# GpSimd's low part of a weight slot: one subtraction of 2048 columns, or four of 512

## The reference, cut to what matters

```
h = rmsnorm(x);  proj = h @ w_in
y_a = rwkv7_time_mix(proj...);  y_b = short_conv(proj...);  y_c = dilated_attention(proj...)
merged = sum_i sigmoid(gate_i) * (y_i @ w_branch[rows_i]);  x += rmsnorm(merged @ w_out)
x += rmsnorm((silu(h @ w_gate) * (h @ w_up)) @ w_ffn_out)
```

## Time and profile before

| what | value |
|---|---|
| median of 3 runs | 1210.95 us (1210.74 to 1216.21) |
| profiled execution | span 1209.4 us; its own time is given only as this span |
| PE | busy 1095.4 us, 91% |
| DVE | busy 595.6 us, 49% |
| ACT | busy 376.8 us, 31% |
| POOL | busy 367.9 us, 30%, of which the 76 subtractions are 357.2 us |
| TensorE clock granted, mean | 0.949 of full speed |

### The profile page before, as it was taken

The page is one execution under the profiler, slowest core; times in us unless marked ns, Lnnn a source line. Parts: engine busy times, 40 slices in busy tenths (PEclk is TensorE's granted clock), DMA queues, the critical chain, the costliest instruction groups (busy, mean ns, idle before and its releaser), DMA issues.

```text
span 1209.4 us, 13739 instructions
## 1 busy us (share of the span) xinstructions
PE 1095.4 (91%) x5541; PEld 898.9 (74%) x5541; DVE 595.6 (49%) x579; ACT 376.8 (31%) x483; POOL 367.9 (30%) x111
## 2 busy tenths in 40 slices
PE   3997999899988998899959979895999999999997
PEld 2886788678867886788747657774888888888885
DVE  5014752875288536853854656524555555550003
ACT  5111412341234123412175353135332233321112
POOL 5343311331133113311330113412434443344331
PEclk8999899989999998999978979996999999999998
DMA  6233121222133113341610154522233233322211
GB/s 202 81 100 104 70 88 53 104 84 74 53 104 104 52 52 104 104 156 60 251 71 1 46 180 157 191 70 70 70 104 103 80 94 104 104 98 77 105 70 70
DMA packets 106750, 116.93 MB, mean 97 GB/s; under 512 B 2462, under 2 KB 86492, under 8 KB 106716
## 3 DMA queue, kind: packets, MB, share of 16 engines
q1 hardware_dynamic: 98080, 99.10, 25.1%
q10 hardware_dynamic: 8636, 17.34, 3.8%
HBM read 100.17 MB, written 16.25 MB: 96 GB/s over the span
## 4 chain that ended last, share of the span: by engine, by line
PE 59%; DVE 17%; issue 17%; POOL 2%; ACT 2%; DMA 0%; ACTq 0%; DVEq 0%; POOLq 0%
PE ps L1187 13%; PE ps L1188 12%; PE ps L1189 12%; PE ps L1277 9%; PE ps L1334 3%; PE ps L1327 3%; POOL w_lo L521 2%; DVE xm L890 2%; DVE bkd L917 2%; DVE y L992 2%; DVE rk L909 1%; DVE sq L911 1%; DVE xm L889 1%; PE ps L1303 1%; PE ps L1312 1%
## 5 line engine op out<-in xcount | busy, mean ns | idle before, releaser
L521 POOL TENSOR_TENSOR w_lo<-w_raw,w_hi 128x2048 fp32r<-128x2048 f32 x76 | 357.2, 4701 | 809.1 <-ACT w_hi L552 809.1
L1187 PE MATMUL ps<-a_hi,w_hi 128*128 128x512 f32 x512 | 201.7, 394 | 8.3 <-DVE a_lo L837 4.5
L552 ACT CAST w_hi<-w_raw 128x2048 fp32r<-128x2048 f32 x76 | 145.0, 1908 | 202.7 <-PE ps L1189 175.9
L1188 PE MATMUL ps<-a_lo,w_hi 128*128 128x512 f32 x512 | 201.0, 393 | 0.0
L1189 PE MATMUL ps<-a_hi,w_lo 128*128 128x512 f32 x512 | 200.9, 392 | 0.0
L1277 PE MATMUL ps<-a_hi,w_hi 128*128 128x512 f32 x384 | 159.7, 416 | 0.0
L1277 PE MATMUL ps<-a_lo,w_hi 128*128 128x512 f32 x384 | 153.3, 399 | 0.0
L1277 PE MATMUL ps<-a_hi,w_lo 128*128 128x512 f32 x384 | 152.3, 397 | 0.0
L1187 PEld LDWEIGHTS ps<-a_hi,w_hi 128*128 128x128 f32 x512 | 97.3, 190 | 29.5 <-issue 9.0
L1188 PEld LDWEIGHTS ps<-a_lo,w_hi 128*128 128x128 f32 x512 | 97.4, 190 | 20.3
L1189 PEld LDWEIGHTS ps<-a_hi,w_lo 128*128 128x128 f32 x512 | 97.2, 190 | 20.3
(11 more groups left out here) (247 smaller groups left out, 1545.7 us busy)
## 6 DMA issues: line engine op xcount, KB each, us to landing
w_raw<-w_in SPq DMA_DIRECT2D x34, 1024.0 KB, 5.0
w_raw<-w_ffn_in SPq DMA_DIRECT2D x44, 512.0 KB, 4.4
spill<-spill_buf ACTq DMA_DIRECT2D x27, 512.0 KB, 2.8
w_raw<-w_ffn_out SPq DMA_DIRECT2D x11, 1024.0 KB, 4.7
w_raw<-w_branch SPq DMA_DIRECT2D x5, 1024.0 KB, 9.2
proj<-spill SPq DMA_DIRECT2D x1, 4608.0 KB, 15.2
g_ab<-spill SPq DMA_DIRECT2D x8, 512.0 KB, 5.7
w_raw<-w_out SPq DMA_DIRECT2D x4, 1024.0 KB, 4.9
```

Of the source, the lines that this page charges most:

```text
L521: g.tensor_tensor(w_lo[:, b], w_raw[:, b], w_hi[:, b].bitcast(F), ALU.subtract).then_inc(lo_ready, 1)
L552: s.copy(w_hi[:, b], w_raw[:, b]).then_inc(hi_ready, 1)
L1187: t_.matmul(dst, w0, a0, start=first, stop=False)
L1188: t_.matmul(dst, w0, a1, start=False, stop=False)
```

## The change

POOL's subtraction of a slot becomes four instructions of 512 columns each, one behind the other. The wait for `hi_ready` stands ahead of the first, the signal `lo_ready` is given by the last.

```diff
+    LO_PARTS = 4
 ...
             def low(n, b):

                 pool.wait_ge(hi_ready, n + 1)
-                g.tensor_tensor(w_lo[:, b], w_raw[:, b], w_hi[:, b].bitcast(F), ALU.subtract).then_inc(lo_ready, 1)
+                for q in range(LO_PARTS):
+                    c = slice(q * SLOT // LO_PARTS, (q + 1) * SLOT // LO_PARTS)
+                    last = g.tensor_tensor(w_lo[:, b, c], w_raw[:, b, c], w_hi[:, b, c].bitcast(F), ALU.subtract)
+                last.then_inc(lo_ready, 1)
```

## The result

The changed kernel takes 1180.99 us (median of 4 runs, 1180.34 to 1183.33), the kernel before 1210.85 us in the same job. The ratio is 0.9744, 95% interval 0.9727 to 0.9761. It is 30 us faster; forecast were 1195.3, with a range from 1187 to 1211. The sign was right, the size was not. The profiled execution has a span of 1179.2 us, 30.2 less than before.

What follows compares the result with a forecast made beforehand. PE, busy 91% of the span, was taken as the bound, others costing only where it waits. Terms summed to 15.6 us off the profiled 1209.4, giving 1193.8, plus 1.55 for the median: 1195.3 us, range 1187 to 1211.

Steps and rivals of the forecast that it cites:

- rival A: POOL's queued piece goes ahead of the waiting DVE operation, so four pieces act as one; say 1213 us; chance 0.15.
- the token shift: DVE's L889 to L891 in each RWKV pass: 0.9 us gained in pass 1, 6.45 in passes 2 to 4.
- L909: DVE operation in each RWKV pass: ending earlier moves L911 up only to its square root; 0.33 us each, 1.3 in all.
- The start: DVE's L843 at the kernel's start ends earlier, but L837 and the last L843 each wait for a piece; 1.0 us gained.
- the merge: Last pair of the merge: L1143 ends 2.05 us earlier and all moves up 1.2; together 3.3 us gained.
- PE's two waits for the low part: PE waits for POOL's part of a slot twice; one lasts 0.3 us longer, a loss of 0.3.
- The clock: Shorter PE waits restore granted clock in the second and fourth pass and merge; half of 7.8 us taken: 3.9 gained.
- The operands: L917 to L925, each RWKV pass: all four pieces fit ahead of L925; no gain, longer pieces lose 1.2 us in all.
- The output: L992 to L998, five two-input DVE operations per RWKV pass: no gain, longer pieces lose 1.2 us in all.
- `y_c`: L1116 ends some 3 us earlier, but L1118 needs PE's spread of the denominators; 1.45 us gained.
- Rival C: Alternation is right, but PE's next wait, at L1303, grows by most of the upstream gain; about 1203 us; chance 0.08.
- Rival B: Pieces are long from fixed cost per POOL instruction; gain used up at 1.53 us, 1220 us at 1.7; chance 0.07.

## Why the prediction was wrong in size

What held: the block of DVE by POOL as the thing that costs, the handover at instruction ends (rival A did not occur), the rule that a place gains what turns fall behind the awaited point, the token shift (8.3 against 7.35), L909, the length of an undisturbed piece (1.25 from start to start against 1.22). The two-part run, which gives 4 us of the 30, confirms the rule. The start (1.1 against 1.0) and the merge (3.4 against 3.0) came out near by luck in part: at the start the chain gave 1.7 and the clock took 0.6; in the merge the last pair gave 2.8 instead of 3.3, and of PE's two waits for the low part one grew by 0.4, near the 0.3 forecast, while the other shrank from 2.3 to 1.4 us, which no term had.

What failed, by its size:
- **The clock**, 10.6 us against 3.9: the largest miss, and the step that failed is that L1303 had no clock term. I had worked out 7.8 and taken half. Behind L1290 in the second and fourth pass 4.1 us came back (2.8 and 1.3) of the 6.2 worked out, in the merge the 1.6. The wait at L1303, 2.6 us in each pass, had its price too, 4.3 us in all (1.3 to 1.5 in three of four passes). The run with the second and third slot alone shows it: the token shift is blocked there as before, and the same 4.3 us come back behind L1303. The last 0.6 is the shift of the lower level against the work, +1.6 and -1.0, which is luck. That a higher clock goes with short waits is what all traces show; why a given wait does or does not lower it is not settled here. In the third pass of before the clock stays up at L1303 behind 2.61 us and falls at L1378 behind 1.83 us.
- **The operands**, 4.4 against -1.2. The step "all four pieces fit ahead of L925" took DVE's and POOL's arrival as in the trace of before. It is right for that phase, as the run with only the third and the sixth slot divided shows (less than 0.1 us per pass). But the L909 term, which I had counted at 0.33 and then put aside, moves DVE ahead by just enough to let L917 in first. I added terms that are not independent.
- **The output**, 1.6 against -1.2. I charged each turn its whole undisturbed length and each DVE operation its own, while in alternation part of each seems to lie under the other's turn: 1.70 us per pair instead of 1.22 + 0.72 = 1.94. The sign named for this term, L992 to L996 near 1.9 us each and L998's end unchanged, came out as 1.5 to 1.7 us and 0.4 us earlier.
- **`y_c`**, 0.3 of the 1.45, and about 1 us lost in attention: the second group of the spread on PE moved 1.1 us less than the first (22.1 against 23.2 us), and L1118 went on waiting for it. The clock did that: it fell about 1 us sooner against the work, so that PE ran more of the spread's products at the lower level. PE's row from 689.40 before, and from the same product at 666.20 after:

```profile
689.40:693.00 3.60, 3.60 (x7) 1.41 (x6) 2.91 (x3) 1.31 (x1) 2.21 (x1) 0.71 0.50 170
```

```profile
666.20:669.80 3.60, 3.60 (x6) 1.51 (x5) 2.81 (x4) 1.31 (x1) 2.21 (x2) 0.55 0.51 168
```

Why it fell sooner is open.

Rival C is contradicted, the wait at L1303 became shorter and not longer. Rival B did not occur with four pieces; its idea, that alternation can be too fine, came true with eight, by PE waiting for the low part, not by the fixed part of a piece.

## What to carry to other kernels

When an operation on one engine now and then takes several times its own length, look for a long instruction of GpSimd that ends just before that operation does. Dividing that instruction gives back only the pieces that fall behind the point someone waits for; count the operations that have to take turns with it up to there. If the low-priority instruction has slack, holding it back with a semaphore wait (two per pass here) until the urgent chain is through gives more than cutting it up (1174.1 against 1181.0 us here), and both together gave 1165.9. Terms of a sum that shift the phase of two engines must be worked out one after another, not added.

## What the runs showed of the hardware that was not expected

- In alternation a turn of a 512-column subtraction costs DVE 1.16 us and of a 256-column one 0.61, where undisturbed pieces follow each other at 1.25 and 0.69 us: by these figures 0.08 to 0.09 us of each hides in the wait.
- POOL's own progress under alternation is slow: 16 pieces that need about 11.2 us alone took 19.2 us beside DVE's chain.
- The granted clock over the window of the RWKV stage went from 0.96 to 0.99 while PE's waits there became 0.4 to 2.4 us shorter; PE's gain by it is 7.4 of the 23.1 us that the stage gave.
